# Value products of 512 weight columns taken from two weight slots, and memory values and keys in alternating halves

## What is computed

```
h = rmsnorm(x, g_mix_pre)
proj = h @ w_in            # fq, fk, fv (512 columns each), 8 gate logits, cq, ck, cv (512 each)
y_fox = forgetting_attention(fq, fk, fv, f_logit)       # 8 heads of 64, causal
y_chk = chunked_relpos_attention(cq, ck, cv, rel_bias)  # 8 heads of 64
x = x + rmsnorm(concat(rmsnorm(y_fox), rmsnorm(y_chk)) @ w_out)
h = rmsnorm(x, g_mem_pre); mem_n = rmsnorm(mem, g_mem_kv)
k = mem_n @ w_mk; v = mem_n @ w_mv                      # 256 memory rows, 4 heads of 256
x = x + rmsnorm(memory_attention(h @ w_mq, k, v) @ w_mo)
```

## Time and profile before

| | |
|---|---|
| median of 3 runs | 2134.06 us (2133.42 to 2136.66) |
| profiled execution, first to last instruction | 2134.6 us |
| mean granted TensorE clock in it | 0.997 |
| TensorE matmul busy | 2083.2 us (98%) |
| VectorE, ScalarE, GpSimd busy | 1235.0, 832.5, 206.5 us |
| bytes read from HBM | 237.75 MB |

### The profile page before, as it was taken

One profiled execution on the slowest core, in us unless ns is written; L12 is line 12 of the kernel. 1 busy time (PEld: TensorE's weight loads), 2 busy tenths in 40 slices (PEclk: granted clock), 3 DMA queues, 4 the chain that ended last, 5 costly groups with the idle time before them and its releaser, 6 DMA issues.

```text
span 2134.6 us, 26510 instructions
## 1 busy us (share of the span) xinstructions
PE 2083.2 (98%) x10728; PEld 1644.9 (77%) x10728; DVE 1235.0 (58%) x1896; ACT 832.5 (39%) x1344; POOL 206.5 (10%) x176
## 2 busy tenths in 40 slices
PE   8999999999999999999999999999999999999998
PEld 7776887678878886666788888787777777888886
DVE  5665756446677777987544344475675755443442
ACT  5344544345323233225423223344464454232232
POOL 1321001011000004453000000100000010000001
PEclk9999999999999999999999999999999999999999
DMA  6322432124777773662233332121221232323321
GB/s 202 97 69 90 137 101 79 34 66 162 254 253 246 268 248 109 166 169 84 94 119 99 99 99 96 56 70 50 60 70 50 70 107 91 105 94 98 99 99 40
DMA packets 218554, 245.51 MB, mean 115 GB/s; under 512 B 9144, under 2 KB 203192, under 8 KB 212288
## 3 DMA queue, kind: packets, MB, share of 16 engines
q1 hardware_dynamic: 208784, 231.73, 33.2%
q10 hardware_dynamic: 9648, 12.08, 2.3%
HBM read 237.75 MB, written 3.78 MB: 113 GB/s over the span
## 4 chain that ended last, share of the span: by engine, by line
PE 88%; DVE 5%; ACT 3%; DMA 1%; issue 1%; ACTq 0%; POOL 0%; SPq 0%; DVEq 0%
PE bank L1323 24%; PE bank L1331 24%; PE bank L1327 24%; PE bank L1348 2%; PE bank L1352 2%; PE bank L1356 2%; PE bank L1457 1%; PE bank L1531 1%; PE bank L1402 1%; PE bank L1508 1%; PE bank L1415 1%; PE bank L1395 1%; PE bank L1440 1%; PE bank L1521 1%; DVE wL L1938 1%
## 5 line engine op out<-in xcount | busy, mean ns | idle before, releaser
L1323 PE MATMUL bank<-hH,wH 128*128 128x512 f32 (+1 forms) x1672 | 634.1, 396 | 18.0 <-ACT wH L1572 8.4
L1331 PE MATMUL bank<-hL,wH 128*128 128x512 f32 (+1 forms) x1672 | 616.8, 386 | 0.0
L1327 PE MATMUL bank<-hH,wL 128*128 128x512 f32 (+1 forms) x1672 | 616.4, 386 | 0.0
L1567 ACT ACTIVATE wH<-raw 128x1024 fp32r<-128x1024 f32 (+1 forms) x376 | 334.2, 939 | 355.7 <-PE bank L1331 283.9
L1938 DVE TENSOR_TENSOR wL<-raw,wH 128x1024 fp32r<-128x1024 f32 (+1 forms) x340 | 375.9, 1142 | 137.0 <-ACT wH L1567 137.0
L1323 PEld LDWEIGHTS bank<-hH,wH 128*128 128x128 f32 x1672 | 313.8, 188 | 109.5 <-issue 29.7
L1331 PEld LDWEIGHTS bank<-hL,wH 128*128 128x128 f32 x1672 | 314.2, 188 | 64.8 <-DVE hL L1958 0.9
L1327 PEld LDWEIGHTS bank<-hH,wL 128*128 128x128 f32 x1672 | 314.5, 188 | 63.6 <-issue 3.1
L1323 PE MATMUL bank<-hidH,wH 128*128 128x512 f32 x768 | 299.1, 389 | 1.9 <-ACT hidH L1729 1.9
L1331 PE MATMUL bank<-hidL,wH 128*128 128x512 f32 x768 | 298.9, 389 | 0.0
L1327 PE MATMUL bank<-hidH,wL 128*128 128x512 f32 x768 | 298.8, 389 | 0.0
(11 more groups left out here) (220 smaller groups left out, 2037.5 us busy)
## 6 DMA issues: line engine op xcount, KB each, us to landing
raw<-in_mlp SPq DMA_DIRECT2D x64, 1024.0 KB, 5.2
araw<-in_ada_w SPq DMA_DIRECT2D x48, 1024.0 KB, 5.0
raw<-in_w_ff SPq DMA_DIRECT2D x32, 1024.0 KB, 7.4
raw<-in_hgrn_in SPq DMA_DIRECT2D x32, 512.0 KB, 3.7
raw<-in_w_in SPq DMA_DIRECT2D x11, 1024.0 KB, 5.3
raw<-in_conv_in SPq DMA_DIRECT2D x16, 512.0 KB, 4.0
u<-conv_u ACTq DMA_DIRECT2D x24, 270.0 KB, 5.1
raw<-in_w_mv SPq DMA_DIRECT2D x4, 1024.0 KB, 5.1
```

The costliest lines, as they stand in the source:

```text
L1323: mm(out, wH[:, s, m:m + 128], xh[:, k, 0:width], start=k == 0, stop=False)
L1327: mm(out, wL[:, s, m:m + 128], xh[:, k, 0:width], start=False, stop=False)
L1331: i = mm(out, wH[:, s, m:m + 128], xl[:, k, 0:width], start=False, stop=k == KB - 1)
L1567: do(wH[:, s, c], raw[:, r, c], ACT.Copy).then_inc(*s_whi.up(n, x))
```

## The change

Three value products go from `linear_tm` to a new function, `wide_tm`. It takes two pieces together and moves 512 columns, 256 from each of two split slots (an access with a step between the slots), so that one matmul takes the place of two, and a full bank is evicted by one ScalarE instruction in place of two. The memory's values and keys, before all values and then all keys, now alternate: values 0 to 511, keys 0 to 511, values 512 to 1023, keys 512 to 1023. Pieces 15 and 16 are thereby of `w_mk`, pieces 17 and 18 of `w_mv`.

```
+    def wide_tm(self, tag, name, k0, c0, ncols, src, ev, width=T):
+        for c in range(0, ncols, 512):
+            n = self.take(name, k0, c0 + c, 256)
+            self.pieces.append((name, k0, c0 + c + 256, 256))
+            for i in range(width // 128):
+                b, after = self.lin.get()
+                part = dict(i=i, b=b, after=after, key=("lin", tag, c, i))
+                for k in range(0, KB, 2):
+                    self.do("lin_wide", n=n, src=src, part=part, ks=(k, k + 1))
+                    if k == 2 and i:
+                        self.lows(1)
+                    if k + 2 == KB:
+                        if i == width // 128 - 1:
+                            self.piece_done[n] = self.piece_done[n + 1] = part["key"]
+                        self.lin.put(b, *ev(tag, i, c, b, part["key"]))
+                    yield 1.0
...
-        run(self.linear_tm("v0", "w_in", 0, 1024, 512, src, to_v(0)))
+        run(self.wide_tm("v0", "w_in", 0, 1024, 512, src, to_v(0)))
...
-            yield from self.linear_tm("v1", "w_in", 0, 2568, 512, src, to_v(1))
+            yield from self.wide_tm("v1", "w_in", 0, 2568, 512, src, to_v(1))
...
-            yield from self.linear_tm("mv", "w_mv", 0, 0, 1024, ("h", "mem"), to_mv, width=256)
-            yield from self.linear("mk", "w_mk", 0, 0, 1024, ("h", "mem"), to_mk, width=256, lag=True)
+            for x in range(2):
+                yield from self.wide_tm(("mv", x), "w_mv", 0, 512 * x, 512, ("h", "mem"), to_mv, width=256)
+                yield from self.linear(("mk", x), "w_mk", 0, 512 * x, 512, ("h", "mem"), to_mk, width=256, lag=True)
...
+                elif kind == "lin_wide":
+                    n, src, p = it["n"], it["src"], it["part"]
+                    xh, xl = operand(src)
+                    out, x = banks[p["b"]][:], slice(128 * p["i"], 128 * p["i"] + 128)
+                    s, step = n % NSPLIT, 2048 * ((n + 1) % NSPLIT - n % NSPLIT)
+                    for k in it["ks"]:
+                        wh, wl = (view(w, 2048 * s + 256 * k, [[step, 2], [1, 256]]) for w in (wH, wL))
...
+                        for m in (n, n + 1):
+                            pe.wait_ge(*s_whi.at(m, quarter(m, k)))
+                        mm(out, xh[:, k, x], wh, start=k == 0, stop=False)
+                        for m in (n, n + 1):
+                            pe.wait_ge(*low(m).at(m, quarter(m, k)))
+                        mm(out, xh[:, k, x], wl, start=False, stop=False)
+                        pe.wait_ge(*s_lo.at(*src[1:], k))
+                        i = mm(out, xl[:, k, x], wh, start=False, stop=k == KB - 1)
...
-                    do(vt[:, g, i, c:c + 256], banks[it["b"]][:, 0:256], ACT.Copy, scale=small[:, 224 + i:225 + i]).then_inc(
-                        *s_act.up("v", g, i, c))
+                    do(vt[:, g, i, :], banks[it["b"]][:], ACT.Copy, scale=small[:, 224 + i:225 + i]).then_inc(
+                        *s_act.up("v", g, i))
```

More of the change, by code:

```diff
@@ L601, in ev @@
             def ev(t, i, c, b, key):
-                do("ev_v", lin=key, g=g, i=i, c=c, b=b)
-                return (("act", "v", g, i, c),)
+                do("ev_v", lin=key, g=g, i=i, b=b)
+                return (("act", "v", g, i),)
             return ev
@@ L645, in to_mk @@
             def to_mk(t, j, b):
-                do("ev_mk", lin=t, j=j, b=b)
-                return (("dve", "mk", j),)
+                do("ev_mk", lin=t, i=j, j=4 * t[1] + j, b=b)
+                return (("dve", "mk", 4 * t[1] + j),)
             def to_mv(t, i, c, b, key):
-                do("ev_mv", lin=key, i=i, c=c, b=b)
-                return (("act", "mv", i, c),)
-            yield from self.linear_tm("mv", "w_mv", 0, 0, 1024, ("h", "mem"), to_mv, width=256)
-            yield from self.linear("mk", "w_mk", 0, 0, 1024, ("h", "mem"), to_mk, width=256, lag=True)
+                do("ev_mv", lin=key, i=i, c=512 * t[1], b=b)
+                return (("act", "mv", i, 512 * t[1]),)
+            for x in range(2):
+                yield from self.wide_tm(("mv", x), "w_mv", 0, 512 * x, 512, ("h", "mem"), to_mv, width=256)
+                yield from self.linear(("mk", x), "w_mk", 0, 512 * x, 512, ("h", "mem"), to_mk, width=256, lag=True)
         alongside(stagger(self.pairs(), 2), rest(), [RW])
@@ L1358, in tensor_program @@
                                 i.then_inc(*s_mm.up(*p["key"]))
+                elif kind == "lin_wide":
[5 more added lines that the diff above has]
+                        wh, wl = (view(w, 2048 * s + 256 * k, [[step, 2], [1, 256]]) for w in (wH, wL))
+                        if k == 0:
+                            for ev in p["after"]:
+                                pe.wait_ge(*event(ev))
+                        pe.wait_ge(*s_hi.at(*src[1:], k))
+                        for m in (n, n + 1):
[6 more added lines that the diff above has]
+                        i = mm(out, xl[:, k, x], wh, start=False, stop=k == KB - 1)
+                        if k == KB - 1:
+                            i.then_inc(*s_mm.up(*p["key"]))
                 elif kind == "close_rows":
@@ L1411, in tensor_program @@
                     for j in range(i + 1):
-                        pe.wait_ge(*s_act.at("v", g, j, 256 * (it["us"][0]["h"] // 4)))
+                        pe.wait_ge(*s_act.at("v", g, j))
                         for u in it["us"]:
@@ L1438, in tensor_program @@
                     for m_ in range(2):
-                        pe.wait_ge(*s_act.at("mv", m_, 256 * h))
+                        pe.wait_ge(*s_act.at("mv", m_, 512 * (h // 2)))
                         m = mm(banks[6 + it["o"]][:], mvv[:, m_, 256 * h + 128 * d:256 * h + 128 * d + 128],
@@ L1624, in scalar_program @@
                 elif kind == "ev_v":
-                    g, i, c = it["g"], it["i"], it["c"]
+                    g, i = it["g"], it["i"]
                     act.wait_ge(*s_mm.at(*it["lin"]))
                     act.wait_ge(*s_act.at("row_rstd", "mix"))
-                    do(vt[:, g, i, c:c + 256], banks[it["b"]][:, 0:256], ACT.Copy, scale=small[:, 224 + i:225 + i]).then_inc(
-                        *s_act.up("v", g, i, c))
+                    do(vt[:, g, i, :], banks[it["b"]][:], ACT.Copy, scale=small[:, 224 + i:225 + i]).then_inc(
+                        *s_act.up("v", g, i))
                 elif kind == "ev_gate":
@@ L1679, in scalar_program @@
                     act.wait_ge(*s_mm.at("out", (0, 3, 3)))
-                    do(mvv[:, i, c:c + 256], banks[it["b"]][:, 0:256], ACT.Copy, scale=mr[:, 256 + i:257 + i]).then_inc(
+                    do(mvv[:, i, c:c + 512], banks[it["b"]][:], ACT.Copy, scale=mr[:, 256 + i:257 + i]).then_inc(
                         *s_act.up("mv", i, c))
@@ L1684, in scalar_program @@
                     act.wait_ge(*s_dve.at("ynorm", j))
-                    act.wait_ge(*s_mm.at("lin", "mk", KB - 1))
+                    act.wait_ge(*s_mm.at("lin", ("mk", 1), 3))
                     do(hH[:, j, :], tmp[:, it["s"], :], ACT.Copy).then_inc(*s_hi.up("y", j))
@@ L2037, in vector_program @@
                     j = it["j"]
-                    dve.wait_ge(*s_mm.at("lin", it["lin"], j))
+                    dve.wait_ge(*s_mm.at("lin", it["lin"], it["i"]))
                     dve.wait_ge(*s_act.at("mr"))
```

## The result

The changed kernel takes 2138.09 us (median of 21 runs, 2135.68 to 2143.10), the kernel before beside it 2134.98 us (median of 21, 2132.59 to 2138.78). The ratio is 1.0014 with the 95% interval 1.0009 to 1.0020: 3.1 us slower, inside the 0.2% that was named as no change, but with an interval that leaves out 1. Forecast were 2137.0 us and +2.9 us. Of the 1.1 us between 2137.0 and 2138.09, 0.9 is the base: the forecast started from 2134.06, the median of three runs of the kernel before.

A forecast was written before the change was run, and what follows sets the result against it. TensorE, busy 98% of the span, was taken as the bound. Terms -3.4 - 0.4 + 0.4 + 1.3 + 3.4 + 1.6 = +2.9 us on the profiled 2134.6 gave 2137.5, as median 2137.0 us; range 2130.3 to 2141.0.

The forecast's parts named there:

- Gain on TensorE: Products of v0, v1 and memory values: 288 of twice the width stream faster than the narrow pairs, 3.4 us saved.
- two runs cost like two products: Rival for the wide products: each 256-column run costs a product, TensorE saves nothing, 2140.4 us; chance 0.08 with the gap rule.
- the gap rule: Wide products: N/2.4 + 2.5 ns between starts, gain 0.7 us, time 2139.7 us; shares the 0.08 chance.
- The stop of 0.60 us: TensorE's wait for a ScalarE copy behind the first memory eviction, which now comes later: gain 0.4 us.
- (a): After v0: the gate rows' store slips from 46.59 to about 57.0, hidden with 2 us left over.
- (b): After v1: a ScalarE copy stands behind one more high-copy pair and a wider eviction, cost 0.4 us.
- (c): First crossing, memory values to keys: held low half of piece 15 delays piece 17's fetch, cost 1.3 us.
- (d): Second crossing, to the keys' second half: held low half of piece 19 delays piece 21, cost 3.4 us.
- The clock: After the second-crossing stop the granted clock falls to 1.2 GHz: 0 to 1.6 us, taken as 1.6.
- covered crossings: Rival: at both crossings pieces 17 and 21 have landed or nothing behind is wanted, 2130.7 us; chance 0.14.
- the longer stops: Rival: low clock also after the first crossing, or gate rows 2 us late, 2138.6 to 2140.6 us; chance 0.18.
- The signs named ahead: At wide memory products' ends: ScalarE waits some 2 and over 3 us for raw, VectorE for wH, fetches late.

The follow-up runs named there:

- e7: Changed kernel with the second high copy and its low halves deferred into the following product after all four wide products: 2137.44 us, kernel before 2137.14.
- e9: Changed kernel with the second high copy and its low halves deferred behind the two wide memory products only: 2131.08 us, kernel before 2135.25.
- e4: Kernel before with only the alternation of memory values and keys by halves, all products 256 wide: 2137.40 us, ratio 1.0003.
- e3: Kernel before with wide memory products and the alternation, v0 and v1 narrow: 2142.21 us, ratio 1.0028.
- e8: Changed kernel with the edits of e7 and e1 together: 2137.98 us, ratio 1.0005 to the kernel before.
- e6: Changed kernel, but a wide memory product puts down no owed low half, both come at the next take: 2143.61 us, kernel before 2137.14.
- e2: Kernel before with wide products for v0 and v1 only, memory left as before: 2135.22 us, kernel before 2136.22.
- e10: e9 with e1's edit added: 2133.37 us, kernel before 2135.25, ratio 0.9994.
- e5: Changed kernel without alternation: both wide value products, then the keys, owed low halves at each wide product's start: 2141.10 us, kernel before 2137.14.
- e1: Changed kernel, but a wide memory product puts down both owed low halves at its second token block: 2135.76 us, kernel before 2136.22.

## Why the prediction held, step by step

- **Gain on TensorE, forecast 3.4 us.** v0 gave 1.29 (A), v1 1.04 (B of e7, where the stop after v1 is absent, 108.17 less 107.13). The memory gave about 1.0: D of e9 is 83.90 with 1.48 us of stops (0.42, 0.50, 0.56), D of before 84.00 with one of 0.60. Together 3.3 us. The rival that two runs cost like two products is dead by the starts 0.2267 us apart. So is the gap rule of the Trainium skill (TensorE: Matmul & The Clock Gate, Back-to-back issue gap), by which 512 columns would start 216 ns apart and the three products would gain 0.7 us; that section gives the rule for a single matmul by itself.
- **The stop of 0.60 us, forecast gain 0.4.** It became 0.43 us and changed its releaser, from ScalarE's copy to `small` of VectorE: a gain of 0.2. In e4, with narrow evictions, it stays at 0.58. The wider eviction did take the copy off the path, and another release was right behind.
- **(a) Gate rows, forecast hidden.** Store at 56.48 (forecast 57.0), first bias at 64.63 (65.2), division over at 70.20 (70.6), first turn at 72.25 (72.8): no stop, and the 2 us of slack were there.
- **(b) After v1, forecast 0.4.** 0.50 measured, 0.49 or 0.50 in six other kernels with the wide v1. It is absent in e3 and e4 (narrow v1) and in e7 and e8, whose list has one high copy fewer at that place.
- **(c) First crossing, forecast 1.3, measured 2.12.** This is the mis-sized term. Counted from the end of the scores at 222.63 the low half of piece 15 started after 1.1 us and ended after 2.3, as forecast; the high halves of 17 started after 7.6 (7.3), and TensorE's values after 11.4 (11.0 and "about 0.2 more"). TensorE was ready for them after 10.5, not 9.9. That gave 0.93 us. The rest, 0.59 at the turn and 0.60 at the scores behind it, I had put at those 0.2 us. VectorE does the reciprocals, the division and the next soft_max one after the other behind the late copy, and TensorE catches up with each of them in turn: it hasn't enough work in between to let VectorE get ahead again. e3 and e6 repeat both (0.6 and 0.6). So the mechanism was right and the price stopped one link too early.
- **(d) Second crossing, forecast 3.4, measured 3.21.** From the end of the scores at 262.80: low half ended after 2.75 us (2.8), piece 21 landed after 7.95 (7.8), VectorE's copy over after 11.9 (11.8), TensorE there after 8.8 (8.4).
- **The clock, forecast 1.6, measured 1.5**, and none after (c), as taken. The reason given, that (d) is longer than the stop that brought it before, doesn't hold up (the last section): that this run drew the low clock here and not after (c) is luck.
- **The sum.** -3.3 -0.2 +0.5 +2.1 +3.2 +1.5 is +3.8, and A+B+D came out at +4.2; 0.3 to 0.4 us are in small stretches that I didn't resolve. The forecast's +2.9 lies nearer to the measured +3.1 than its parts lie to theirs, and that closeness is luck: C and the rest of the span differ by more than that between two profiles.

Of the rivals, covered crossings fell to the stops themselves. Of the longer stops, the one that came is (c) alone, and for another reason than the clock or the gate rows. The signs named ahead all appeared: both fetches were issued only after the low half (225.03 and 265.62), ScalarE waited 1.95 and 3.40 us for `raw`, VectorE 0.99 and 3.05 us for `wH`.

What stays open is the size of e2 and e4 in the medians: by A, B and D they should be 1.8 us faster and level, and the medians say 1.0 us faster and 1.2 slower. The intervals, some 2 us to each side, hold both.

## What to carry to other kernels

When a wider instruction frees two buffers at once, the load it held back is late. Most of the cost isn't in that but in the place of its consumer in an in-order list: put it behind the work that TensorE wants first, or put the last reader of the old buffer earlier. Then look again at every place where the moved instruction now stands. The same deferral that took 4.2 us of stops away behind the memory products lengthened the stop behind v1 by 2.5 us, because it stood ahead of the instruction that releases the memory loads. And when a stop is computed, follow it past its first link: the instructions that the late one holds back stop the fast engine once more each, until there is enough work between them.

## What the runs showed of the hardware

- **The low clock after a stop isn't decided by the stop's length alone.** It came after stops of 1.94 us (e2), 2.00 us (the changed kernel) and 2.24 us (e10), and not after 1.97 us (e3), 2.42 us (e4) or 2.49 us (e6), all at the same place and doing the same work. The windows of e2:

```profile
192.00:194.00 2.00, 1.36 (x13) 0.73 0.03 8
194.00:196.00 2.00, 2.00 (x10) 0.50 0.11 12
```

and of e4:

```profile
194.00:196.00 2.00, 0.80 (x12) 1.00 0.01 4
196.00:198.00 2.00, 2.00 (x15) 1.00 0.04 4
```

  So the forecast's term of 1.6 us was a chance and not a certainty. It was drawn behind (d) in the changed kernel, and behind both crossings in e3 and e6.
- **Much of the scatter between runs goes with the mean granted clock.** In the series of e9, the kernel before's runs with a mean clock of 0.998 took 2133.5 us (4 runs), at 0.997 2134.4 (8), at 0.996 2136.0 (7), at 0.995 2138.0 (2): 4.5 us over 0.003. In the series of e5 to e8 it shows less clearly: 2135.0, 2136.8, 2137.9 and 2137.5 us. Eight of e9's eleven runs were at 0.998, four of the kernel before's 21. That fewer stops are the reason isn't shown: e10, whose stops outside the memory loads are no longer than e9's, had two of eleven there.
- **The stop at the memory loads is set by when the memory rows land.** It was 1.08 and 1.10 us in e1 and e9 and 1.7 to 2.5 us in the others that have that code. ScalarE squares the memory's rows as they land (`tmp<-qk`), and the high copy and then the copy of `PTb` that TensorE wants stand behind this. In the changed kernel ScalarE waited for them again on the way:

```profile
188.91 1.53 ACT L1701 ACTIVATE tmp<-qk 128x256 f32<-128x256 f32 x4 [0.82 <-DMA qk<-in_mem]
190.35 1.99 ACT L1607 ACTIVATE wH<-raw 128x1024 fp32r<-128x1024 f32 x2
```

  In e9 it did seven in one go, all landed:

```profile
187.19 2.56 ACT L1706 ACTIVATE tmp<-qk 128x256 f32<-128x256 f32 x7
189.65 1.99 ACT L1612 ACTIVATE wH<-raw 128x1024 fp32r<-128x1024 f32 x2
```

  From the issue of the loads of `rel` to that high copy it is 8.23 us in e1 (181.39 to 189.62), 8.24 in e9, 8.88 in e5, 9.08 in e2, 9.12 in e3, 9.15 in the changed kernel, 9.39 in e10, 9.57 in e4, 9.60 in the kernel before and 9.63 in e6. Less 7.15 us, each is TensorE's stop in that profile to 0.01 us. Why the rows land sooner in one execution than in another isn't known.
